# Sparse-attention stage of a decoder trunk: one weight unit split earlier in its own buffers, a scaling and a transpose moved between projection tiles, and the middle block's index dots issued two a tile

## What is computed

```python
def dsa_attention(h, w_in, q_norm, kv_norm, w_uq, w_qidx, kidx_g, kidx_b, w_uk, w_uv, w_out):
    c_q, c_kv, k_idx, w_idx = jnp.split(h @ w_in, [256, 512, 576], axis=-1)
    c_q = rmsnorm(c_q, q_norm)
    c_kv = rmsnorm(c_kv, kv_norm)
    k_idx = layernorm(k_idx, kidx_g, kidx_b)
    w_idx = w_idx * (HI ** -0.5)
    def block(args):
        q_idx = (cq_b @ w_qidx).reshape(B, Q_BLOCK, HI, DI)
        dots = jnp.einsum('bthd,bsd->btsh', q_idx, k_idx) * (DI ** -0.5)
        score = jnp.einsum('btsh,bth->bts', jax.nn.relu(dots), w_b)
        score = jnp.where(causal[None], score, -jnp.inf)
        _, sel = lax.top_k(score, top_k)
        ...
    return out @ w_out
```

## Time and profile before

| what | before |
|---|---|
| median of 3 runs | 2015.93 us (2015.18 to 2016.17) |
| the profiled execution | 2017.32 us, of which its span is 2015.4 us |
| TensorE busy | 1976.4 us, 98% of the span |
| VectorE busy | 1352.6 us, 67% |
| ScalarE busy | 843.9 us, 42% |
| GpSimd busy | 251.8 us, 12% |
| mean granted TensorE clock | 0.992 |

### The profile page before, as it was taken

The page is one execution under the profiler, slowest core; times in us unless marked ns, Lnnn a source line. Parts: engine busy times, 40 slices in busy tenths (PEclk is TensorE's granted clock), DMA queues, the critical chain, the costliest instruction groups (busy, mean ns, idle before and its releaser), DMA issues.

```text
span 2015.4 us, 23546 instructions
## 1 busy us (share of the span) xinstructions
PE 1976.4 (98%) x9246; PEld 1636.4 (81%) x9246; DVE 1352.6 (67%) x1692; ACT 843.9 (42%) x1145; POOL 251.8 (12%) x186
## 2 busy tenths in 40 slices
PE   8999999999999999999999999999998999999997
PEld 7788888877878788888888888888887888888886
DVE  6999944433534446999944799984367659999732
ACT  5545632232222223555531555562157445455510
POOL 0000012010010141000011000002135540000021
PEclk9999999999999999999999999999999999999998
DMA  4234122323222232233132333223222014322221
GB/s 167 84 105 146 54 104 96 118 68 104 77 80 84 84 105 84 84 128 123 58 103 69 126 120 132 84 86 101 81 84 84 1 43 144 106 84 98 101 95 62
DMA packets 69721, 189.49 MB, mean 94 GB/s; under 512 B 4016, under 2 KB 12208, under 8 KB 64496
## 3 DMA queue, kind: packets, MB, share of 16 engines
q1 hardware_dynamic: 69376, 187.25, 26.7%
q0 software_dynamic: 240, 0.79, 0.1%
HBM read 185.92 MB, written 2.10 MB: 93 GB/s over the span
## 4 chain that ended last, share of the span: by engine, by line
PE 87%; DVE 7%; issue 3%; ACT 2%; POOL 1%; DMA 0%; SPq 0%; POOLq 0%; DVEq 0%; ACTq 0%
PE bank L1899 13%; PE bank L1901 13%; PE bank L1900 13%; PE bank L1907 13%; PE bank L1909 12%; PE bank L1908 12%; PE bank L2116 2%; PE bank L1913 2%; PE bank L1915 2%; PE bank L1914 2%; PE bank L2006 2%; DVE part_lo L1248 1%; PE bank L2106 1%; PE bank L2250 1%; PE bank L2305 1%
## 5 line engine op out<-in xcount | busy, mean ns | idle before, releaser
L815 ACT ACTIVATE part_hi<-quad_w 128x1024 fp32r<-128x1024 f32 x280 | 293.1, 1063 | 281.5 <-PE bank L1909 202.2
L1248 DVE TENSOR_TENSOR part_lo<-quad_w,part_hi 128x1024 fp32r<-128x1024 f32 x280 | 330.2, 1218 | 27.8 <-ACT part_hi L815 27.4
L1899 PE MATMUL bank<-gated_hi,out_hi 128*128 128x512 f32 x704 | 274.6, 390 | 0.0
L1901 PE MATMUL bank<-gated_hi,out_lo 128*128 128x512 f32 x704 | 273.9, 389 | 0.0
L1900 PE MATMUL bank<-gated_lo,out_hi 128*128 128x512 f32 x704 | 273.9, 389 | 0.0
L1907 PE MATMUL bank<-part_hi,s_hi 128*128 128x512 f32 x640 | 252.3, 394 | 2.1 <-DVE part_lo L1248 2.1
L1909 PE MATMUL bank<-part_hi,s_lo 128*128 128x512 f32 x640 | 249.4, 390 | 0.0
L1908 PE MATMUL bank<-part_lo,s_hi 128*128 128x512 f32 x640 | 249.2, 389 | 0.0
L1907 PE MATMUL bank<-part_hi,xn_hi 128*128 128x512 f32 x608 | 239.3, 394 | 5.7 <-DVE part_lo L1248 5.7
L1909 PE MATMUL bank<-part_hi,xn_lo 128*128 128x512 f32 x608 | 238.1, 392 | 0.0
L1908 PE MATMUL bank<-part_lo,xn_hi 128*128 128x512 f32 x608 | 238.1, 392 | 0.0
(11 more groups left out here) (235 smaller groups left out, 3334.0 us busy)
## 6 DMA issues: line engine op xcount, KB each, us to landing
quad_w<-w_ffn_in SPq DMA_DIRECT2D x80, 1024.0 KB, 7.3
out_raw<-w_ffn_out SPq DMA_DIRECT2D x64, 704.0 KB, 4.1
w_raw<-w_ret_in SPq DMA_DIRECT2D x24, 1024.0 KB, 4.8
rest_raw<-w_ffn_in SPq DMA_DIRECT2D x32, 256.0 KB, 5.2
w_raw<-w_ret_out SPq DMA_DIRECT2D x8, 1024.0 KB, 4.8
w_raw<-w_dsa SPq DMA_DIRECT2D x8, 1024.0 KB, 4.8
x_res<-x_in SPq DMA_DIRECT2D x8, 256.0 KB, 6.1
out<-x_res SPq DMA_DIRECT2D x8, 256.0 KB, 2.2
```

The source lines that it names most:

```text
L815: nc.scalar.activation(in_four(part_hi[part_slot(h)]), source, copy).then_inc(part_hi_made, 1)
L1248: nc.vector.tensor_tensor(in_four(part_lo[part_slot(h)]), source, in_four(part_hi[part_slot(h)]).bitcast(FP32), ALU.subtract)\
L1899: mm(to, w_hi_of[:, at:at + width], hi, start=start, stop=False)
L1901: return mm(to, w_lo_of[:, at:at + width], hi, start=False, stop=stop)
```

## The change

In the dsa sublayer alone:

- `w_uq` moves from unit 5 to unit 2 and gets a raw buffer of its own, `uq_raw`; the halves of the keys' latents become units 3 and 4, the index queries' weights unit 5. `DSA_SLOTS` says which buffer each unit uses, `DSA_FREE` what its high part waits for. ACT splits units 2 and 3 one after the other; POOL makes `uq_lo` ahead of its two inverse roots; DVE makes unit 3's low part behind `k_twice`.
- ACT's four scalings of the keys' latents move from before the tile loop to behind tile 1, TensorE's turning of them from tile 4 to tile 3, ACT's copies of the turned parts from tile 5 to 4, DVE's from round 12 of the first block's selection to behind that selection.
- `dots_behind(j)`: tiles 0 to 3 have two dots each (the middle block's eight), tiles 4 to 11 one each (the last block's eight). `weigh` and `relu` follow.
- Unit 6's high part (ACT) moves from before the tile loop to behind tile 5, unit 7's from behind tile 7 to behind tile 11, and POOL's low parts of units 6 and 7 stand behind the middle and behind the last block's additions.
- `minimum(0)` and `minimum(1)` stand behind two of the four early rounds, not behind all four. `EARLY_OUT` is 17 (was 18), and `ROUNDS_AT` has one round at step 11 for those at 10 and 12, and a second one at step 17.

```diff
-DSA_SIZES = [CHUNKS * IDX_COLS, UNIT, UNIT // 2, UNIT // 2, RANK // P * IDX_HEADS * IDX_DIM] \
-    + [UNIT] * (3 + DSA_OUT_UNITS)
+DSA_SIZES = [CHUNKS * IDX_COLS, UNIT, UNIT, UNIT // 2, UNIT // 2, RANK // P * IDX_HEADS * IDX_DIM] \
+    + [UNIT] * (2 + DSA_OUT_UNITS)
+DSA_SLOTS = (0, 1, 2, 0, 1, 0, 0, 1, 0, 1, 0, 1)
+DSA_FREE = (None, None, 0, 1, 2, 3, 5, 5, 5, 5, 7, 8)
...
-    ROUNDS_AT = {8: 1, 10: 1, 12: 1, 14: 1, 16: 1, 17: 1, 18: 2, 19: 2, 20: 2}
+    ROUNDS_AT = {8: 1, 11: 1, 14: 1, 16: 1, 17: 2, 18: 2, 19: 2, 20: 2}
-    EARLY_OUT = 18
+    EARLY_OUT = 17
+    DOT_TILES = 3 * IDX_HEADS // 2
+    def dots_behind(j):
+        if j < IDX_HEADS // 2:
+            return range(IDX_HEADS + 2 * j, IDX_HEADS + 2 * j + 2)
+        return range(j + 3 * IDX_HEADS // 2, j + 3 * IDX_HEADS // 2 + 1) if j < DOT_TILES else range(0)
...
 -                    (load_first if n < 2 else load)(u0 + n, source)
+                    if n < 2:
+                        load_first(u0 + n, source)
+                        continue
+                    if n == 2:
+                        sp.wait_ge(unit_done, u0)
+                    else:
+                        sp.wait_ge(w_lo_made, u0 + max(m for m in range(n) if DSA_SLOTS[m] == DSA_SLOTS[n]) + 1)
+                    sp.dma_start(unit_bufs(u0 + n)[0][:, :source.shape[-1]], source)\
+                        .then_inc(raw_loaded[DSA_SLOTS[n]], 16)
...
 +                split_unit(u0 + 2)
                 inverse_rms_3(0, 1)
                 inverse_rms_3(1, 0)
-                split_unit(u0 + 5)
...
-                    if n < 2:
-                        split_unit(u0 + POOL_SPLITS[0] + n)
-                split_unit(u0 + POOL_SPLITS[0] + 2)
-                split_unit(u0 + POOL_SPLITS[0] + 3)
+                    if n == 1:
+                        split_unit(u0 + POOL_SPLITS[0])
+                for n in range(1, 4):
+                    split_unit(u0 + POOL_SPLITS[0] + n)
...
                  split_unit(u0 + 2)
+                split_unit(u0 + 3)
...
-                act.wait_ge(r_col3_done, 4)
-                for b in range(BLOCKS):
-                    nc.scalar.activation(cols(latents, BLOCKS + b, RANK), latent_columns(1, b), copy,
-                                         scale=r_col3[:, 2 * BLOCKS + b:2 * BLOCKS + b + 1])\
-                        .then_inc(latents_scaled, 1)
-                split_unit(u0 + 6)
...
-                    if 0 < j <= 16:
-                        weigh(IDX_HEADS + j - 1)
-                    if j < 16:
-                        relu(IDX_HEADS + j)
-                    if j == 5:
+                    for c in dots_behind(j):
+                        if c > IDX_HEADS:
+                            weigh(c - 1)
+                        relu(c)
+                    if j == DOT_TILES:
+                        weigh(len(DOTS) - 1)
+                    if j == 1:
+                        scale_key_latents()
+                    elif j == 4:
                         latent_parts(1)
-                    if j % 8 == 7 and j < 23:
-                        split_unit(u0 + 7 + j // 8)
-                    elif j == 19:
-                        split_unit(u0 + 9)
+                    elif j == 5:
+                        split_unit(u0 + 6)
+                    elif j in (11, 15, 19):
+                        split_unit(u0 + 7 + (j - 11) // 4)
...
 -                split_unit(u0 + 2)
...
+                dve.wait_ge(w_lo_made, u0 + 3)
+                split_unit(u0 + 3)
...
                     find_8(first_block)
                     mark_8(first_block)
-                    if n == 11:
-                        latent_parts(1)
                 choice_to_bias(first_block)
+                latent_parts(1)
...
                 for n in range(EARLY_ROUNDS):
                     find_8(last_block)
                     mark_8(last_block)
-                minimum(0)
-                minimum(1)
+                    if n == EARLY_ROUNDS // 2 - 1:
+                        minimum(0)
+                        minimum(1)
...
                      if kk == 0:
-                        pe.wait_ge(w_lo_made, u0 + 3 + half)
+                        pe.wait_ge(w_lo_made, u0 + 4 + half)
...
-                    if j % 8 == 0:
+                    if j % 8 == 0 and j > 0:
                         pe.wait_ge(w_lo_made, u0 + 6 + j // 8)
...
-                    if j < 16:
-                        dots(IDX_HEADS + j)
-                    if j == 4:
+                    for c in dots_behind(j):
+                        dots(c)
+                    if j == 3:
                         turn_latents(1)
```

More of the change, by code:

```diff
@@ L300, in build @@
     decay_loaded, decay_reloaded = sem("decay_loaded"), sem("decay_reloaded")
-    raw_loaded = [sem(f"raw_loaded{n}") for n in range(2)]
+    raw_loaded = [sem(f"raw_loaded{n}") for n in range(2)] + [sem("uq_loaded")]
     w_hi_made, w_lo_made = sem("w_hi_made"), sem("w_lo_made")
@@ L429, in unit_bufs @@
             return out_raw[n], out_hi[n], out_lo[n]
[L430 to L434, removed]
+        if SUBLAYERS[s] == "dsa":
+            n = u - FIRST_UNIT[s]
+            m = n - (DSA_UNITS - DSA_OUT_UNITS)
+            slot = DSA_SLOTS[n]
+            if n == 2:
+                return uq_raw, uq_hi, uq_lo
+            if 0 <= m < 2:
+                return (w_raw[slot],) + dsa_out_parts[m]
+            return w_raw[slot], w_hi[slot], w_lo[slot]
         return w_raw[u % 2], w_hi[u % 2], w_lo[u % 2]
@@ L452, in unit_loads @@
         before = sum(UNITS_OF[k] for k in SUBLAYERS[:s] if k != "ffn")
+        if SUBLAYERS[s] == "dsa":
+            slot = DSA_SLOTS[n]
+            return raw_loaded[slot], 16 * ((before // 2 if slot < 2 else 0) + DSA_SLOTS[:n + 1].count(slot))
         return raw_loaded[n % 2], 16 * (before // 2 + n // 2 + 1)
@@ L649, in _ @@
                 half, idx = UNIT // 2, DSA_SIZES[0]
-                sources = [w_dsa_idx[:, :idx], w_dsa[0], w_dsa[1][:, :half], w_dsa[1][:, half:],
-                           w_dsa_idx[:, idx:]] + [w_dsa[n] for n in range(2, 5 + DSA_OUT_UNITS)]
+                sources = [w_dsa_idx[:, :idx], w_dsa[0], w_dsa[2], w_dsa[1][:, :half], w_dsa[1][:, half:],
+                           w_dsa_idx[:, idx:]] + [w_dsa[n] for n in range(3, 5 + DSA_OUT_UNITS)]
                 for n, source in enumerate(sources):
-                    (load_first if n < 2 else load)(u0 + n, source)
+                    if n < 2:
+                        load_first(u0 + n, source)
+                        continue
+                    if n == 2:
+                        sp.wait_ge(unit_done, u0)
[3 more added lines that the diff above has]
+                        .then_inc(raw_loaded[DSA_SLOTS[n]], 16)
         for k in range(CHUNKS):
@@ L801, in split_unit @@
             act.wait_ge(loaded, count + 16 * pair)
-            if SUBLAYERS[stage_of(u)] == "dsa" and n >= DSA_UNITS - DSA_OUT_UNITS:
-                act.wait_ge(unit_done, u - 3)
-            elif n >= 2 and SUBLAYERS[stage_of(u)] != "ffn" and (SUBLAYERS[stage_of(u)], n) != ("dsa", 5):
+            if SUBLAYERS[stage_of(u)] == "dsa":
+                if n >= 2:
+                    act.wait_ge(unit_done, FIRST_UNIT[stage_of(u)] + DSA_FREE[n])
+            elif n >= 2 and SUBLAYERS[stage_of(u)] != "ffn":
                 act.wait_ge(unit_done, u - 1 + 2 * pair)
@@ L1154, in _, with scale_key_latents @@
                 square_latents(1)
-                act.wait_ge(r_col3_done, 4)
-                for b in range(BLOCKS):
-                    nc.scalar.activation(cols(latents, BLOCKS + b, RANK), latent_columns(1, b), copy,
-                                         scale=r_col3[:, 2 * BLOCKS + b:2 * BLOCKS + b + 1])\
-                        .then_inc(latents_scaled, 1)
-                split_unit(u0 + 6)
+                def scale_key_latents():
+                    act.wait_ge(r_col3_done, 4)
+                    for b in range(BLOCKS):
+                        nc.scalar.activation(cols(latents, BLOCKS + b, RANK), latent_columns(1, b), copy,
+                                             scale=r_col3[:, 2 * BLOCKS + b:2 * BLOCKS + b + 1])\
+                            .then_inc(latents_scaled, 1)
                 def exps(i):
```

16 lines of the change are left out of this document (8 added, 8 removed).

## The result

| | median | runs | range |
|---|---|---|---|
| before | 2015.78 us | 6 | 2015.08 to 2016.37 |
| changed | 2026.42 us | 6 | 2024.53 to 2028.17 |

The changed kernel takes 1.0052 times as long, 95% interval 1.0041 to 1.0062: 10.6 us more. Forecast were +7.6 us, 2023.5, in a range of 2017 to 2027.

The account below looks back on a forecast made before the run. The prediction took TensorE, holding 87% of the chain, as the bound, so only its waits count. 4.8 (keys' latents) + 3.3 (attention's start) - 0.5 (attention steps) = +7.6 us on 2015.93 gave 2023.5, range 2017 to 2027.

Parts of the forecast that it names:

- what the change takes away: VectorE's 5.59 us break in selection and TensorE's 3.93 us wait at tile 2; alone a gain, priced at 9 us.
- the three places: Where TensorE was forecast to wait anew: at the keys' latents, before tile 8 and before tile 16.
- faster: Rival: units 6's and 7's low parts come in time, attention starts 9.0 us earlier, 2006.9 or 2011.7 us; chance 0.12.
- First place: Keys' latents: GpSimd's `uq_lo` split holds VectorE's centring; TensorE waits 3.9 us, 3.4 of it new, plus 1.4 clock: 4.8.
- the other order: Rival at the keys' latents: centring not held or ahead of GpSimd's split, costing 1.4 to 2.1 us; chance 0.15.
- Second place: Tile 8: TensorE waits 4.6 us for unit 6's low part, then loses 1.7 us of clock.
- Third place: Tile 16: TensorE waits 4.3 us more for unit 7's low part, and again loses 1.7 us of clock.
- tile 14's 0.5: At tile 14 TensorE loses 0.5 us, as its bank waits for tile 12's copy.
- Start of attention: Attention waits for `logits(1)` and starts at 1558.5 instead of 1555.23: 3.3 us later, besides the 4.8 at the keys' latents.
- Attention steps: Fewer rounds in steps 8 to 16 gain up to 1.5 us, step 17's product waits up to 1.5: -0.5 taken.
- Sum: All terms together: 4.8 + 3.3 - 0.5 = +7.6 us, a forecast median of 2023.5; chance 0.55.

Follow-up runs that it names:

- e8: e7 with the attention steps of before (old selection rounds, output products from step 18); 2007.49 us.
- e6: The changed kernel, but GpSimd makes `uq_lo` only behind VectorE's last low part of the index weights; 2022.73 us.
- e1: The changed kernel, but GpSimd makes `uq_lo`, with its own semaphore, only when the queries' latents are scaled; 2026.08 us.
- e2: e1 without the wait for `latents_scaled`, so GpSimd starts `uq_lo` right behind the second inverse root; 2023.17 us.
- e5: The kernel before with only the change's attention steps (its `ROUNDS_AT`, and output products from step 17); 2019.56 us.
- e7: The changed kernel with the edits of e6 and e3 together, attention steps as changed; 2010.70 us.
- e9: e8 with output products from step 17; 2009.34 us.
- e10: e8 with the change's selection rounds, output products still from step 18; 2008.21 us.
- e12: The changed kernel with the centring as a `scalar_tensor_tensor` that adds a tile of zeros; 2026.27 us in one execution.
- e3: The changed kernel, unit 6's high part between the first block's relus, its low part before the middle block's additions, unit 7's parts where unit 6's were; 2014.82 us.
- e11: The changed kernel with e6's edit and unit 6's parts early, unit 7 as changed; 2016.53 us.
- e4: The changed kernel with `EARLY_OUT` back to 18; 2025.66 us.

## Why the prediction was right, and where not

- **What bounds the kernel, and what the change takes away.** Right. With the three places mended, attention starts 8.2 us earlier (forecast in the rival "faster": 9.0, 2006.9 us; e8 has 2007.5).
- **First place.** Forecast 4.8 us, measured 5.5 at the first dot. The hold was right, and the wait close (3.45 us for 3.9; in both 0.5 replaces the old one). That GpSimd's split got ahead of the centring was a matter of 0.09 us; the forecast gave the other order 0.15. The mis-sized term is the clock: 1.4 us, where the window has 5 x 0.46 = 2.3 and another half microsecond ahead of it: 2.8. It had been cut down because part of it would fall beside VectorE's work, and TensorE was busy all through it. Of the whole kernel's time the place costs 3.7 us (e6). The kind of instruction that is held was put down too loosely (e1, e2), without effect on the sum.
- **Second place.** Wait 4.6 forecast, 4.64 measured. Clock 1.7, measured 1.4 here. Tile 8 started at 1522.5 + 4.8 = 1527.3 by the forecast, and at 1525.83 + 2.12 = 1527.95.
- **Third place.** Wait 4.3, measured 3.85; tile 14's 0.5, measured 0.67. `logits(1)` was forecast at 1554.2 + 4.8 = 1559.0 and came at 1557.59 + 2.12 = 1559.7.
- **Start of attention.** Together +8.1, measured +8.65. By the experiments' medians, which hold the clock too, the three places cost 3.7 + 6.2 + 5.8 = 15.7 us, where I counted 17 (the terms as listed there add up to 17.6).
- **Attention steps.** This term failed: -0.5, with bounds of 1.5 either way, where e5 has +4.1 and e7 against e8 +3.2 (+2.4 between attention and end in the changed kernel's own trace, whose clock did not fall behind the wait). The step's wait for the results' parts was named, with 1.5 us as the upper bound; it is 1.9, and its clock, which e5 and e7 paid and the changed kernel and e9 did not pay on top, was left out. The other half is the overlap: fewer rounds in steps 8 to 16 were to gain up to 1.5 us, and in e10 the new rounds leave TensorE idle 1.5 us more. I took a mean between a gain that does not exist and a loss put too low.
- **Sum.** Gain 8.3, against 15.7 and 3.2 lost: +10.6, all in medians (2015.8 - 8.3 + 18.9 = 2026.4; the parts were taken away one after another, so they add up by construction). The forecast was 3.0 short: 0.6 ahead of attention, the rest in the attention steps. The number fell inside the range although this term had the wrong sign.

## What to carry to other kernels

When a low-priority job is moved back to make room for an urgent one, give it a due time: here two weight splits, of 4.6 us each on the slow engine, went from ten and six microseconds early to some four late, and cost 12 of the 19 us that turned a change worth 8 us into a loss of 11. Cost a long wait of TensorE with low clock behind it: every wait of 3.4 us or more in this stage, in all the traces here, was followed by 1.4 to 3.1 us of it. Behind waits of 1.9 to 2.8 us it came in 14 cases of 23, so there only the length of the wait is certain. And before an instruction with two on-chip inputs is put beside a long GpSimd one, look at what stands within its 4.6 us on VectorE: moving the GpSimd instruction from one place to another may only choose another victim.

## What the runs showed of the hardware that was not expected

- The hold works both ways, by who starts first: 4.09 us for 1.4 on VectorE, 5.53 us for 4.6 on GpSimd, in the same run (e1).
- Reading a bank frees a VectorE `tensor_scalar` from it (1.90 us beside GpSimd's split in e2); with two SBUF inputs even a `scalar_tensor_tensor` is held (5.20 us in e12).
- The length of a shorter wait does not settle what clock follows. Behind the same wait of 1.9 us at the first early output product the clock fell in seven traces (e1, e3, e5, e6, e7, e9, e11; to 0.66 in e5 and e9) and not at all in three (the changed kernel, e2, e12). Behind the wait of 2.2 to 2.6 us at the first transposes it fell in the changed kernel, e2, e4, e7, e8, e10 and e12, and not in e1, e3, e6, e9 and e11. Only e7 had both, and e5, whose first wait is 6.32 us. So two traces of nearly the same kernel can have the same loss in different places, and a window of one is no measure of what an edit cost. Behind 2.83 us in e1 the clock stayed at 1.00, in the window of 1485 and in this one:

```profile
1490.00:1495.00 5.00, 4.89 (x32) 4.69 (x31) 2.49 (x5) 2.91 (x7) 0.00 (x0) 1.00 0.92 364
```

The changed kernel's own window behind its wait, which ended at 1588.53:

```profile
1590.00:1595.00 5.00, 5.00 (x41) 4.74 (x41) 3.83 (x11) 2.89 (x4) 2.71 (x2) 1.00 0.00 0
```

This variation is a likely source of the changed kernel's wider spread, 3.6 us against 1.3; that was not tested.
